# Two small SBUF tiles placed in front of the large ones in a one-core, two-block transformer kernel

## What is computed

```python
# first block
h = rmsnorm(x); proj = h @ w_in                      # q,k,v | rwkv columns | gates
o_att  = dilated_window_attention(q, k, v)           # 12 heads, dilations 1, 4, 16
o_rwkv = rwkv7_time_mix(token_shift(f_rwkv), ...)    # 16 heads of 64, a recurrence over tokens
merged = gate0 * (o_att @ w_att_branch) + gate1 * (o_rwkv @ w_rwkv_branch)
x = x + rmsnorm(merged @ w_out)
x = x + rmsnorm(square(relu(rmsnorm(x) @ w_ffn1)) @ w_ffn2)       # 1024 -> 4096 -> 1024
# second block
u = rms_norm(h); proj = u @ w_in_2
merged = sigmoid(g_pool) * y_pool + sigmoid(g_attn) * y_attn      # pooling, windowed attention
h = h + merged @ w_out_2
h = h + (silu(u2 @ w_gate) * (u2 @ w_up)) @ w_down                # 1024 -> 2816 -> 1024
return rms_norm(h)
```

## Time and profile before

| | us |
|---|---|
| median of 3 executions | 1761.08 |
| lowest, highest | 1760.17, 1761.31 |
| the profiled execution | 1761.03 |
| its span, first to last instruction | 1759.2 |

### The profile page before, as it was taken

How to read it: one execution, slowest core, us unless ns; L and a number is a source line. 1 busy time by engine, 2 the same in 40 slices (tenths; PEclk the granted TensorE clock), 3 DMA queues, 4 the chain that set the end, 5 groups by cost and what they waited for, 6 DMA issues and landing times.

```text
span 1759.2 us, 22211 instructions
## 1 busy us (share of the span) xinstructions
PE 1738.5 (99%) x9392; PEld 1436.4 (82%) x9392; DVE 839.6 (48%) x1195; ACT 724.5 (41%) x1092; POOL 503.0 (29%) x126
## 2 busy tenths in 40 slices
PE   9999999999999999999999999999999999999998
PEld 8898778888888888888888888877778888888887
DVE  3015477998989754251124443627844411123343
ACT  5244555655566452352232223536652522222222
POOL 2442300000000003524444444233344244444442
PEclk9999999999999999999999999999999999999999
DMA  5432231110011124432222222322222222222221
GB/s 199 165 125 72 93 99 57 28 52 25 28 39 38 37 104 148 143 108 96 96 96 96 96 96 96 115 87 72 73 96 96 93 100 101 100 97 96 96 96 72
DMA packets 57238, 159.46 MB, mean 91 GB/s; under 512 B 3471, under 2 KB 35087, under 8 KB 42548
## 3 DMA queue, kind: packets, MB, share of 16 engines
q1 hardware_dynamic: 45132, 137.64, 22.8%
q10 hardware_dynamic: 12008, 20.40, 3.4%
HBM read 150.41 MB, written 9.19 MB: 91 GB/s over the span
## 4 chain that ended last, share of the span: by engine, by line
PE 91%; DVE 4%; ACT 3%; DMA 1%; issue 1%; POOL 0%; ACTq 0%; SPq 0%; DVEq 0%
PE ps L654 26%; PE ps L656 24%; PE ps L655 24%; PE ps L1128 2%; PE ps L1213 1%; PE ps L1116 1%; ACT ht_hi L1507 1%; PE ps L1171 1%; PE ps L1136 1%; DMA w_raw<-in_wpack 1%; PE ps L1045 1%; PE ps L1161 1%; PE ps L840 1%; PE ps L1181 1%; PE ps L873 1%
## 5 line engine op out<-in xcount | busy, mean ns | idle before, releaser
L645 POOL TENSOR_TENSOR w_lo<-w_raw,w_hi 128x2048 fp32r<-128x2048 f32 (+2 forms) x122 | 502.8, 4127 | 1229.3 <-ACT w_hi L1472 1206.8
L654 PE MATMUL ps<-ht_hi,w_hi 128*128 128x512 f32 (+1 forms) x1312 | 524.6, 400 | 3.7 <-DVE ht_lo L2252 3.4
L656 PE MATMUL ps<-ht_hi,w_lo 128*128 128x512 f32 (+1 forms) x1312 | 499.6, 381 | 0.0
L655 PE MATMUL ps<-ht_lo,w_hi 128*128 128x512 f32 (+1 forms) x1312 | 498.8, 380 | 0.0
L1472 ACT ACTIVATE w_hi<-w_raw 128x2048 fp32r<-128x2048 f32 x125 | 239.3, 1915 | 453.7 <-PE ps L656 400.6
L654 PEld LDWEIGHTS ps<-ht_hi,w_hi 128*128 128x128 f32 x1312 | 247.4, 189 | 63.7 <-issue 18.0
L656 PEld LDWEIGHTS ps<-ht_hi,w_lo 128*128 128x128 f32 x1312 | 247.1, 188 | 48.7
L655 PEld LDWEIGHTS ps<-ht_lo,w_hi 128*128 128x128 f32 x1312 | 247.8, 189 | 39.4 <-issue 1.9
L2853 DVE TENSOR_TENSOR hid_lo<-hidden,hid_hi 128x1024 fp32r<-128x1024 f32 x27 | 129.3, 4788 | 149.1 <-ACT hid_hi L2050 149.1
L654 PE MATMUL ps<-w_hi,hid_hi 128*128 128x512 f32 x432 | 168.2, 389 | 0.0
L656 PE MATMUL ps<-w_hi,hid_lo 128*128 128x512 f32 x432 | 168.1, 389 | 0.0
(11 more groups left out here) (354 smaller groups left out, 2353.1 us busy)
## 6 DMA issues: line engine op xcount, KB each, us to landing
w_raw<-in_wpack SPq DMA_DIRECT2D x113, 1024.0 KB, 4.8
w_raw<-in_wpack SPq DMA_DIRECT2D x26, 512.0 KB, 5.2
x_res<-in_x SPq DMA_DIRECT2D x4, 512.0 KB, 6.2
gate_back<-gate_dram ACTq DMA_DIRECT2D x2, 1024.0 KB, 6.7
gate<-gate_dram ACTq DMA_DIRECT2D x1, 2048.0 KB, 8.5
x_res<-in_x ACTq DMA_DIRECT2D x1, 2048.0 KB, 7.9
bias_skewed_dram<-bias_rows_dram ACTq DMA_DIRECT2D x1, 1792.0 KB, 10.5
gate_dram<-rwkv_out ACTq DMA_DIRECT2D x6, 256.0 KB, 3.5
```

What stands on the lines that cost most here:

```text
L645: last = nc.gpsimd.tensor_tensor(Wl[:, slot, cc], raw[:, slot, cc], f32(Wh[:, slot, cc]), ALU.subtract)
L654: mm(dst, wh, ah, start=first, stop=False)
L655: mm(dst, wh, al, start=False, stop=False)
L656: return mm(dst, wl, ah, start=False, stop=last)
```

## The change

Two tiles, `one_less_mu` (104 bytes, 128 with rounding) and `stat` (256 bytes), get their places ahead of `x_res` instead of behind `params_sb`. Nothing else is edited.

```diff
@@ -250,6 +250,8 @@
             return ctx.enter_context(nc.semaphore(name))
 
 
+        OM = fixed("one_less_mu", [P, 26])
+        stat = fixed("stat", [P, 64])
         Xr = fixed("x_res", [P, NT, D])
         x_at = top[0] - 4 * NT * D
         Y = fixed("y_tok", [P, NT, D])
@@ -263,8 +265,6 @@
         Wh = fixed("w_hi", [P, RING, UNIT], F32R)
         C = fixed("consts", [P, N_EARLY_CCOLS])
         PR = fixed("params_sb", [P, N_PCOLS])
-        OM = fixed("one_less_mu", [P, 26])
-        stat = fixed("stat", [P, 64])
         OAT = fixed("att_out", [P, 2, T])
```

## The result

The changed kernel takes 1768.62 us (median of 5, 1767.55 to 1769.40) against 1761.08 us for the kernel before in the same session (median of 5, 1760.17 to 1763.60): ratio 1.0042, 95% interval 1.0031 to 1.0054. It is 7.5 us slower. The forecast was no difference, at 1760.9 us, and the time lies above its range. The case that came true is the rival called "the two operands drift apart", which had a chance of 0.04.

The account below looks back on a forecast made before the run. TensorE, busy for 1738.5 of 1759.2 us, was taken to bound the kernel. From 1761.1 us, 0.1 for the start's loads and 0.1 for the load at 1356 us gave 1760.9 us, range 1757.6 to 1763.5.

Parts of the forecast that it names:

- the two operands drift apart: FFN-down: `w_hi` and `hid` end 128 bytes apart, slowing 1296 products; 17.2 us if the fixed part doubled, 1778; chance 0.04.
- I take 0 ns for all three engines.: VectorE, ScalarE and TensorE instructions on moved tiles keep their times; TensorE bounded at 1 ns either way per matmul.
- The slower rival: FFN-down products slow as their operands' offsets come to differ; decides from 2.7 ns each, priced at 13.3, 1778 us; chance 0.04.
- The faster rival: 4608 matmuls lose part of their 13.3 ns fixed cost once operands are aligned; all of it gives 1700 us; chance 0.05.
- The 16-byte rule: SBUF accesses: only crossing into a new 16-byte line costs, so starts at 128 and 0 are equally good, worth nothing.
- The half units: 26 half-unit weight loads, landing in 5.2 us, should change most, to 5.2 us or below, without effect on the time.
- 3% off a whole unit: Whole-unit weight loads: 33 transactions become 32 if the rule for reads holds for these writes; 0.2 us at 2.59 and 1356.
- The two single loads: First weight unit at 2.59 us and a late load at 1356 us; 0.1 us of gain taken for the start and for 1356.
- The load at 1356 us: Late weight load, 7.01 us against a median of 4.8; 0.1 us of gain taken, between -0.5 and +0.5.
- the 0.5 us wait: TensorE's single weight-load wait for a `w_lo` from GpSimd, following the load at 1356 us; caps that load's gain at 0.5 us.
- The slowed stretch behind 232 us: TensorE's granted clock drops after its wait for `kb`, losing 1.7 us; 0 change taken, 1.7 us kept on both sides.

Follow-up runs that it names:

- the bursts: TensorE alone, the whole computation left out, 60 products per pair of operand offsets; 512 columns took 226.7 ns a step at 0/0, 233.3 with the moving operand 192 ahead.
- the three variants of the kernel before: The kernel before with only the FFN's hidden tiles begun 384, 256 or 192 bytes later: 1767.20, 1760.90 and 1763.80 us.
- the five variants: Kernel before, hidden tiles 384, 256, 192 bytes later: 1767.20, 1760.90, 1763.80 us; changed kernel, hidden tiles 384 later: 1761.27, or every large tile at a multiple of 256: 1761.33.

## Why the prediction was wrong

*What bounds the kernel.* Right. TensorE is busy for 99% before and after, and the 7.5 us came out of the matmuls themselves, from the part on top of the columns: 226.7 - 213.3 = 13.3 ns before and 19.1 in FFN-down after. The prediction had named this as the only part that an address might touch. It also called this part the same whatever the length, from rows of 256 and 512 columns; the bursts don't bear that out. At 128 columns 57.5 ns come on top of the columns (110.8 - 53.3), and at 256 columns with the moving operand 192 ahead only 7.1.

*"I take 0 ns for all three engines."* This is the step that failed, for TensorE: the term was 0 ns, bounded at 1 ns a product, and it measured 5.7 ns on the 1296 products with `hid`, 7.4 us. For the other engines it held on tiles that moved: VectorE's multiply on `gate` 1222 ns before and after, ScalarE's rounding into `w_hi` 1916 and 1914, GpSimd's `w_lo` 4604 and 4605. The 0 rested on `consts` with `y_tok` against `consts` with `kb`, 273 ns each. Those products have 128 columns, and the bursts show what such a row can tell: 110.8 against 111.7 ns, when 512 columns at the same distances give 226.7 and 233.3. They are also transposes of plain float32 tiles, and the moving `consts` at 128 is 64 ahead of `kb` at 320 modulo 256, the distance that costs least of the three (2.5 ns at 512 columns). The row was the nearest in the trace, but not of the form whose cost was at stake. All 512-column float32r rows of before had equal offsets and could show nothing. Also, it was read from durations, which hardly move even where the pace does: 389 to 393 ns for a step that went from 226.7 to 232.4.

*The slower rival.* Its mechanism is what happened: the loss is confined to products with one moved and one unmoved operand, and down is slower while up keeps its pace. The price of the loss was 5.7 ns, above the 2.7 ns from which it decides and under the 13.3 at which it had been priced, so 1768.6 and not 1778. It left out the products with `att` and `yp_hi` (0.9 us by the traces), and it spoke of the distance as such where the distance modulo 256 counts. The chance of 0.04 came from the 128-column row alone. Without it the trace said nothing on the form in question; the chance should then have been several times larger, and the range should have reached to it.

*The faster rival.* Excluded by the runs: 0/0, 128/128 and 320/320 take 226.7 to 227.5 ns. Absolute alignment gives nothing that shows.

*The 16-byte rule of the Trainium skill* (SBUF — State Buffer, the box on SBUF "cachelines") says that SBUF has lines of 16 bytes and that crossing into a new one costs; it was taken to mean that starts at 128 and 0 are equally good. For one operand by itself that agrees with the bursts at equal offsets; as a statement on a product's two operands it doesn't: multiples of 64 bytes at different offsets cost up to 6.6 ns here. The measurement decides.

*DMA.* The half units landed in 5.0 us instead of 5.2, without effect, as predicted; the whole ones unchanged at 4.8. The medians of all seven profiles agree: 4.9 to 5.0 us for half units in the three kernels with `w_raw` at 0, 5.1 to 5.4 in the four with it at 128, and 4.8 for whole units in every one. The estimate from the Trainium skill (DMA: Bandwidth & Descriptors, "How a descriptor splits into AXI transactions") of 3% off a whole unit isn't seen in the medians, which have a resolution of 2%.

The two single loads that the sum rested on moved by more than the sum gave them, but not with the address. The first unit landed 7.29 us after its issue instead of 6.65, and as the second residual tile came 0.7 us later too, the first half of `w_hi` began at 9.91 us instead of 9.27; with `w_raw` left at 128, the three variants of the kernel before have 7.05 to 7.25. The load at 1356 us took 7.01 us in the profile before and 5.86 in the one after (issued at 1360.65), and the 0.5 us wait is gone. It took 6.05 to 6.15 in those three variants, again without a wait. So the long load belongs to one execution, and the sum had counted it as a property of the kernel. Nor were two loads issued in one go there, as the prediction has it: the next followed at 1367.13.

*The clock.* The slowed stretch behind 232 us is absent in the profiled execution after (granted 1.00 from 228 to 240 us, for 0.52 and 0.63 in the earlier trace rows) and in four of the five variants, and present again in the kernel with the hidden tiles at 320 (0.84 over 230 to 235 us and 0.82 over 235 to 240). It comes and goes between executions of kernels that do the same work there, so keeping 1.7 us for it on both sides was right. TensorE's wait of 2.1 to 2.2 us ahead of it is in the executions with and without the slowed clock alike, so that wait alone doesn't decide it. How much of the scatter between executions it makes isn't shown, as only one of each kernel was traced.

## What to carry to other kernels

Before moving a tile, list which matmuls read it together with a tile that stays: for 512-column float32r products the two operands' start addresses should be equal modulo 256 bytes, and moving both together changed nothing here. When a row is used as a bound, it must be of the same shape and type as the instructions that it stands for, and the pace must be read from start to start. A bottleneck engine at 99% turned 2.5% on products that fill a sixth of its time into 0.4% of the whole, so a rival on that engine deserves more than a few per cent as long as no such row speaks.

## What was not expected of the hardware

TensorE's pace depends on the distance of its two operands in SBUF, for multiples of 64 bytes modulo 256, with no other engine at work: 226.7 ns at 0, 229.2 at 64, 232.5 at 128, 233.3 at 192, for 128x128 by 512 in float32r. At 0 and at 192 every step is the same to 1 ns; at 128 the steps run from 228 to 241 ns in a pattern that comes back every seven products. For 256 columns the order is turned round, 120.0 ns at 0 and 113.8 at 192. The kernel has 672 products of that length with `ht` and `w`, 384 with `ht` moving and 288 with `w` moving. A shift of 192 for the first is one of 64 for the others (117.7 ns in the same kernel of bursts), so an estimate of the most that this could give is 384 x 6.2 + 288 x 2.3 ns = 3.0 us. It wasn't tried, since the same tiles serve the 512-column products, for which 192 is the worst of the four.
